# Bias of the masked softmax on ScalarE with v copied out first; the second block's value products moved and cut by token block

## The reference, cut to what matters

```python
# first block, per query block of 128 (dsa_attention)
rel   = relu(einsum('bqhd,bsd->bqhs', qi, ki))
score = einsum('bqh,bqhs->bqs', wi, rel)
score = where(visible, score, -inf)
_, idx = top_k(score, 128)
p = softmax(where(valid, (q @ k[idx]) * scale, -inf));  y_attn = p @ v[idx]
...
# second block (keys: 512 tokens and 16 meta tokens)
# out_a: 8 query heads over 2 key heads, plain softmax
p = softmax(qa @ ka * scale);  out_a = p @ va
# out_b: 4 heads, each with two softmaxes over the keys
p = softmax(qb @ kb * scale)                # two per head
w = p[:, :, 0] - lam * p[:, :, 1]
out_b = rms_norm(w @ vb, subln_g) * (1 - lam_init)
x = x + concat([out_a, out_b]) @ w_out      # then the feed-forward part
```

## Time and profile before

| what | value |
|---|---|
| median of 3 runs | 2317.85 us (2316.51 to 2325.55) |
| the profiled execution, its own time | 2319.75 us |
| its span | 2317.6 us |
| busy: PE, PEld, DVE, ACT, POOL | 98%, 78%, 44%, 26%, 63% |
| weight chunks loaded | 350 of 512 KB |

### The profile page before, as it was taken

The page is one execution under the profiler, slowest core; times in us unless marked ns, Lnnn a source line. Parts: engine busy times, 40 slices in busy tenths (PEclk is TensorE's granted clock), DMA queues, the critical chain, the costliest instruction groups (busy, mean ns, idle before and its releaser), DMA issues.

```text
span 2317.6 us, 30711 instructions
## 1 busy us (share of the span) xinstructions
PE 2261.8 (98%) x11027; PEld 1819.0 (78%) x11027; DVE 1016.3 (44%) x1568; ACT 609.1 (26%) x1081; POOL 1466.5 (63%) x1452
## 2 busy tenths in 40 slices
PE   8999999999999999999999999999999889999999
PEld 7767887888888887778878888888887557888887
DVE  6975654533321049658545332311483554323200
ACT  4333324221110023243242211110334553111100
POOL 6644765876766756548658676667492246766763
PEclk9999999999999999999999999999999999999999
DMA  5321233322222233213343222222320102222222
GB/s 184 100 73 55 96 109 123 127 91 100 96 94 100 94 113 105 68 56 102 103 141 117 94 97 93 100 91 100 119 106 10 37 1 91 93 98 100 93 98 82
DMA packets 69859, 217.35 MB, mean 94 GB/s; under 512 B 8448, under 2 KB 10752, under 8 KB 69632
## 3 DMA queue, kind: packets, MB, share of 16 engines
q1 hardware_dynamic: 54016, 188.41, 24.4%
q10 hardware_dynamic: 15744, 27.52, 3.3%
HBM read 195.93 MB, written 10.49 MB: 89 GB/s over the span
## 4 chain that ended last, share of the span: by engine, by line
PE 90%; DVE 6%; ACT 2%; issue 1%; DMA 0%; ACTq 0%; POOL 0%; DVEq 0%; POOLq 0%
PE ps L1673 79%; PE ps L2167 2%; PE ps L2000 1%; DVE score L1453 1%; DVE small L1449 1%; PE ps L1939 1%; ACT pe L1017 1%; PE ps L1924 1%; PE ps L2227 1%; PE ps L2229 1%; PE ps L2187 1%; PE ps L1952 1%; PE ps L1987 0%; PE ps L2030 0%; PE ps L2096 0%
## 5 line engine op out<-in xcount | busy, mean ns | idle before, releaser
L536 POOL TENSOR_TENSOR w_lo<-w_raw,w_hi 128x512 fp32r<-128x512 f32 x700 | 954.1, 1363 | 58.4
L533 POOL TENSOR_SCALAR w_hi<-w_raw 128x512 fp32r<-128x512 f32 x700 | 491.4, 702 | 658.6 <-DMA w_raw<-wst 628.4
L1673 PE MATMUL ps<-h_hi,w_lo 128*128 128x512 f32 (+1 forms) x2056 | 804.5, 391 | 18.7 <-ACT v_sb L786 4.0
L1673 PE MATMUL ps<-h_hi,w_hi 128*128 128x512 f32 (+1 forms) x2056 | 785.1, 382 | 0.0
L1673 PE MATMUL ps<-h_lo,w_hi 128*128 128x512 f32 (+1 forms) x2056 | 785.0, 382 | 0.0
L1673 PEld LDWEIGHTS ps<-h_hi,w_lo 128*128 128x128 f32 x2056 | 387.8, 189 | 120.4 <-issue 33.0
L1673 PEld LDWEIGHTS ps<-h_lo,w_hi 128*128 128x128 f32 x2056 | 387.9, 189 | 78.4 <-issue 6.7
L1673 PEld LDWEIGHTS ps<-h_hi,w_hi 128*128 128x128 f32 x2056 | 387.6, 189 | 75.0
L1673 PE MATMUL ps<-a_hi,w_lo 128*128 128x512 f32 (+1 forms) x572 | 213.7, 374 | 0.0
L1673 PE MATMUL ps<-a_hi,w_hi 128*128 128x512 f32 (+1 forms) x572 | 213.2, 373 | 0.0
L1673 PE MATMUL ps<-a_lo,w_hi 128*128 128x512 f32 (+1 forms) x572 | 213.2, 373 | 0.0
(11 more groups left out here) (304 smaller groups left out, 2535.4 us busy)
## 6 DMA issues: line engine op xcount, KB each, us to landing
w_raw<-wst SPq DMA_DIRECT2D x350, 512.0 KB, 3.5
rot<-raw ACTq DMA_DIRECT2D x70, 128.0 KB, 3.2
gates<-gt ACTq DMA_DIRECT2D x32, 256.0 KB, 4.1
stage<-gates ACTq DMA_DIRECT2D x32, 256.0 KB, 3.6
x_sb<-xin SPq DMA_DIRECT2D x8, 256.0 KB, 5.4
out<-x_sb SPq DMA_DIRECT2D x8, 256.0 KB, 4.5
kc<-cst ACTq DMA_DIRECT2D x1, 1056.0 KB, 5.1
kc<-cst SPq DMA_DIRECT2D x1, 417.0 KB, 8.0
```

What stands on the lines that cost most here:

```text
L533: eng.tensor_scalar(w_hi[s][:, part], w_raw[s][:, part], 1.0, 1.0, ALU.mult, ALU.mult)\
L536: eng.tensor_tensor(w_lo[s][:, part], w_raw[s][:, part], w_hi[s][:, part].bitcast(F32), ALU.subtract)\
L1673: m = eng.matmul(o, w, x, start=first and i == 0, stop=final and i == 2)
```

## The change

Four things:

1. In the first block ACT copies v0 to v3 out ahead of `qk_norm(7)` instead of behind it.
2. The bias is made on ACT, as Relu(score x 5e-9 + 1e30), so 1e30 where a key was not kept and 0 where it was; DVE subtracts it. It stands ahead of the copy of f3 and waits for the last MATCH_REPLACE (`topk_done`); DVE's first reduction of each query block waits for it (`bias_ready`). The copy of the causal mask is on ACT too.
3. In the second block the pieces of `VB_FILLS` are spread otherwise: steps 0 to 4 have 3, 3, 1, 1, 0 of them (before 4, 4, 3, 3, 2), steps 6 to 12 have the same number as before, and steps 14 to 16 have 2, 3, 3 (before none). The values of units 4 to 7 are multiplied by one query block at a time, one block per step (`values_differential`).
4. `kept_split` comes 4 steps later (t = 19 to 21, before 15 to 17), and `result_lower` of these one step behind it instead of in the same step. The output projection takes k in the order 3, 0, 1, 2, 4, ...

```diff
-VB_FILLS = {0: (1, range(0, 4)), 1: (1, range(4, 8)), 2: (2, range(0, 3)), 3: (2, range(3, 6)), 4: (2, range(6, 8)),
...
+VB_FILLS = {0: (1, range(0, 3)), 1: (1, range(3, 6)), 2: (1, range(6, 7)), 3: (1, range(7, 8)),
...
+            14: (4, range(0, 2)), 15: (4, range(2, 5)), 16: (4, range(5, 8))}
+KEPT_AT = TB * PAIRS_A + 3
+SPLIT_ORDER = [3, 0, 1, 2, 4, 5, 6, 7]
...
+def values_before(u, b):
+
+    return 2 * u + b // 2 + 1 if u < PAIRS_A else 2 * PAIRS_A + TB * (u - PAIRS_A) + b + 1
...
-                qk_norm(7)
                 for t in range(TB):
                     free(eng.activation(v_sb[:, t, :], acc((l, f"v{t}")), ACT.Copy), (l, f"v{t}"))
+                qk_norm(7)
+
+                def bias(b):
+
+                    dst = bias_t[:, BOFF[b]:BOFF[b] + NKEYS[b]]
+                    if b == 0:
+                        eng.activation(dst, causal, ACT.Copy, scale=-1.0).then_inc(bias_ready, 1)
+                        return
+                    eng.wait_ge(topk_done, 3 * l + b)
+                    eng.activation(dst, score[:, b - 1, 0:NKEYS[b]], ACT.Relu, scale=NEG / -2.0e38, bias=far)\
+                       .then_inc(bias_ready, 1)
+
                 for i in range(4):
+                    if i == 3:
+                        for b in range(TB):
+                            bias(b)
                     free(eng.activation(f_sb[:, i, :], acc((l, f"f{i}")), ACT.Copy), (l, f"f{i}"))
...
-                for b in (1, 2, 3):
-                    after(last[b])
-                    k = step(eng.tensor_scalar(bias_t[:, BOFF[b]:BOFF[b] + NKEYS[b]], score[:, b - 1, 0:NKEYS[b]],
-                                               -2.0e38, NEG, ALU.is_gt, ALU.mult))
-                after(k)
...
+                        if p == 0 and i == 0:
+                            eng.wait_ge(bias_ready, 4 * l + b + 1)
...
-                    eng.wait_ge(v2_done, 2 * u - 1 + b // 2)
+                    eng.wait_ge(v2_done, values_before(u - 1, b))
...
-                if 0 <= t - TB * PAIRS_A + 1 < KEPT:
-                    kept_split(t - TB * PAIRS_A + 1)
+                if 0 <= t - KEPT_AT < KEPT:
+                    kept_split(t - KEPT_AT)
...
-                if 0 <= t - TB * PAIRS_A + 1 < KEPT:
-                    result_lower(t - TB * PAIRS_A + 1)
+                if 0 <= t - KEPT_AT - 1 < KEPT:
+                    result_lower(t - KEPT_AT - 1)
...
+            def values_differential(u, b):
+
+                eng.wait_ge(t2_taken[b % 2], turns_before(u) + b // 2 + 1)
+                if b == 0 and u == PAIRS_A:
+                    eng.wait_ge(ysp_lo, 8 * L2 + 1)
+                    taken(eng, (L2, "vbm"))
+                elif b == 0:
+                    eng.wait_ge(y2_taken, u - PAIRS_A)
+                cols = slice((u - PAIRS_A) * P, (u - PAIRS_A + 1) * P)
+                toks = slice(b * P, (b + 1) * P)
+                y = bank(7)
+                for kb in range(TB):
+                    m = eng.matmul(y[:, toks], vb_sb[:, kb, cols], pt2[0][:, kb, toks], start=b + kb == 0, stop=False)
+                m.then_inc(v2_done, 1)
+                if b == TB - 1:
+                    eng.wait_ge(tm_taken, u + 1)
+                    eng.matmul(y, vbm_sb[0:META, cols], ptm[0:META, :], start=False, stop=True).then_inc(y2_ready, 1)
...
-                if b == 0 and u > 0:
+                if b == 0 and 0 < u <= PAIRS_A:
                     values(u - 1, 1)
-                if b == 2 and u >= 0 and u < UNITS:
+                if b == 2 and 0 <= u < PAIRS_A:
                     values(u, 0)
+                if t - LAG - 1 >= TB * PAIRS_A:
+                    values_differential(*divmod(t - LAG - 1, TB))
```

More of the change, by code:

```diff
@@ L1096, in _ @@
             step(eng.memset(eps, EPS))
+            step(eng.memset(far, -NEG))
             eng.wait_ge(in_dma, 32)
@@ L1445, in _ @@
                 for i in range(8):
-                    for _ in range(2):
+                    for j in (2 * i, 2 * i + 1):
                         for b in (1, 2, 3):
@@ L1452, in _ @@
                             s = score[:, b - 1, 0:NKEYS[b]]
-                            last[b] = step(eng.match_replace(s, m8[b], s, MARK))
-                    rope(3 + i)
-                for b in (1, 2, 3):
-                    after(last[b])
-                    k = step(eng.tensor_scalar(bias_t[:, BOFF[b]:BOFF[b] + NKEYS[b]], score[:, b - 1, 0:NKEYS[b]],
-                                               -2.0e38, NEG, ALU.is_gt, ALU.mult))
-                after(k)
+                            ins = eng.match_replace(s, m8[b], s, MARK)
+                            if j == TOPK // 8 - 1:
+                                ins.then_inc(topk_done, 1)
+                            else:
+                                last[b] = step(ins)
+                    rope(3 + i)
                 for p in range(PAIRS_1):
@@ L2206, in values @@
                 for i in range(2):
-                    eng.wait_ge(t2_taken[i], turns_before(u) + (2 * j + 2 if u < PAIRS_A else j + 1))
+                    eng.wait_ge(t2_taken[i], turns_before(u) + 2 * j + 2)
                 if j:
@@ L2212, in values @@
                     eng.wait_ge(vz_dma, 16)
-                elif u <= KEPT:
+                else:
                     eng.wait_ge(y2_kept, u)
[L2215 to L2219, removed]
                 rows = [slice(64 * i, 64 * i + 64) for i in range(2)]
-                cols = slice((u - PAIRS_A) * P, (u - PAIRS_A + 1) * P)
                 toks = HALVES[j]
@@ L2224, in values @@
                 for kb in range(TB):
[L2225 to L2229, removed]
+                    for i in range(2):
+                        m = eng.matmul(y[rows[i], toks], va_sb[:, kb, rows[i]], pt2[i][:, kb, toks], start=j + kb == 0, stop=False)
                 m.then_inc(v2_done, 1)
-                if j == 0:
-                    return
-                if u < PAIRS_A:
+                if j:
                     for i in range(2):
                         m = eng.matmul(y[rows[i]], vmz[0:2 * META, rows[i]], ptm[0:2 * META, :], start=False, stop=True)
-                else:
-                    m = eng.matmul(y, vbm_sb[0:META, cols], ptm[0:META, :], start=False, stop=True)
-                m.then_inc(y2_ready, 1)
+                    m.then_inc(y2_ready, 1)
+            def values_differential(u, b):
[14 more added lines that the diff above has]
+                    eng.matmul(y, vbm_sb[0:META, cols], ptm[0:META, :], start=False, stop=True).then_inc(y2_ready, 1)
             def o_square_2(h):
@@ L2264, in _ @@
             cs = [chunk((L2, f"wo{i}")) for i in range(4)]
-            for k in range(KT):
-                if k == 2:
+            for n, k in enumerate(SPLIT_ORDER):
+                if n == 2:
                     o_square_2(HH - 1)
-                eng.wait_ge(ysp_lo, 8 * L2 + k + 1)
+                eng.wait_ge(ysp_lo, 8 * L2 + n + 1)
                 for i in range(4):
-                    m = product(bank(i), *weights(cs[i], k), h_hi[:, k, :], h_lo[:, k, :], k == 0, k == KT - 1)
-                    if k == KT - 1:
+                    m = product(bank(i), *weights(cs[i], k), h_hi[:, k, :], h_lo[:, k, :], n == 0, n == KT - 1)
+                    if n == KT - 1:
                         m.then_inc(w_used, 1)
```

23 lines of the change are left out of this document (13 added, 10 removed).

## The result

The changed kernel takes 2304.36 us (median of 6, 2301.65 to 2307.34) against 2318.61 of the kernel before (median of 6), a ratio of 0.9937 with a 95% interval of 0.9923 to 0.9951. The forecast was 2304.4. The profiled execution has a span of 2303.3 us; that of before had 2317.6.

The account below looks back on a forecast made before the run. PE, with 90% of the span, was taken to bound the kernel. Gains of 2.4 (layer 0), 3.1 (layer 1) and 8.0 (second block) sum to 13.5 us, from 2317.85 to 2304.4, range 2300.5 to 2310.5.

Parts of the forecast that it names:

- Early steps +4.1: Second block's attention, steps 0 to 4: with fewer value pieces they take 18.2 us against 22.4, a gain of 4.1.
- Steps 14 and 15 -2.1: Second block's attention: two and three value pieces more in these steps cost 1.40 and 0.74 us, a loss of 2.1.
- Steps 16 and 17 -0.1: Second block's attention: step 16 with three more pieces plus step 17 at the floor, 9.74 us against 9.63.
- Step 18 +1.6: Second block's attention: DVE's copy no longer stands behind ACT's split, so a 1.58 us wait goes, gain 1.6.
- Steps 21 to 31 +1.8: Values by blocks: meta-key steps gain 1.0, steps behind lose 0.5 to 0.6; +0.4 in two units, +1.0 at step 30.
- The loop's end (+1.0): Behind the attention loop: only one value block left before the output projection, gain 1.0 us, from -0.5 to 1.6.
- layer 0 (2.4 of 4.0): First block, layer 0: fill(0) earlier by 2.4 us if the clock falls again as before, 4.0 if not.
- layer 1 (3.1): First block, layer 1: PE's wait for v and the half-clock stretch behind it go, scores 3.1 us earlier.
- Step 20: Second block's attention: 5.25 us with values at half clock becomes 3.5 with values by blocks, gain 1.7.
- the clock case: Rival: new half-clock stretches behind waits in both layers and at the loop's end, gain 9.5 to 12, about 2306.9; chance 0.24.
- the dear blocks: Rival: narrow value blocks in the second block's attention cost 1.92 us each, time 2314.7, halfway 2310; chance 0.08.
- the slower case: Rival: PE held at the lower clock in the later attention steps, 30 us over fifteen steps, 2334; chance 0.05.

Follow-up runs that it names:

- e1_layers: Kernel before with items 1 and 2 alone (v copied first, bias on ACT in the first block): 2312.78 us, ratio 0.9974.
- e9_projection_in_gap: Changed kernel with twelve matmuls of the output projection's tile 0 put into PE's wait at the loop's end: 2299.30 us, ratio to before 0.9919.
- e12_no_spread: Changed kernel with the table of value pieces (VB_FILLS) of the kernel before: 2305.34 us, ratio 0.9939.
- e10_after_again: The changed kernel itself, the same program measured once more: 2302.95 us (2301.38 to 2304.32).
- e7_late_split: Kernel before with item 4 alone (later splits): 2314.97 us, ratio 0.9976.
- e3_v_first: Kernel before with v copied out ahead of qk_norm(7), bias still on VectorE: 2317.22 us, ratio 0.9989.

## Why the prediction was right

The total (13.5 forecast, 14.3 measured) is right, and so are these terms singly. Early steps +4.1: 3.99. Steps 14 and 15 -2.1: -2.12. Steps 16 and 17 -0.1: -0.09. Step 18 +1.6: 1.65. Steps 21 to 31 +1.8: 2.21, though by two errors that cancel in part: the steps with the meta keys gave 0.84 each for the 1.0, and those behind them lost 0.14 for the 0.5 to 0.6. And the value block, taken at 0.9 from the earlier trace rows with 1.92 as its upper bound: 1.00 from its start to that of the transposes, 1877.96 to 1878.96. The Trainium skill's spacings (TensorE: Matmul & The Clock Gate, section on the back-to-back issue gap), from which the prediction had estimated a block near 1.92, did not carry over to these float32 products.

The loop's end (+1.0) reads 0.62 in the two profiles. Over the traces step 31 to the projection takes 15.2 to 16.4 us with two blocks, 15.6 on average, and 14.6 to 14.7 with single ones: 0.9, as forecast. What the prediction put at nothing is the half-clock stretch that ran on behind the projection's start in three of the six older traces (21.0 us from there to the residual in all others, 22.3 to 23.7 in these), another 0.9 on average.

Three steps hold less than the total suggests.

*The clock in the two layers.* I let the half-clock stretch stand in layer 0 (2.4 of 4.0) and fall away in layer 1 (3.1). The trace had it the other way round: 3.76 and 1.65. That their sum is right, 5.4 against 5.5, is luck of the execution. The mistake is not the choice of layer, but that I chose by layer at all. The traces show that it comes and goes with the execution: in the five traces that have both edits and an unsplit fill(0) (the changed kernel twice, e1, e9, e12), rope to fill is 2.9 eight times of ten and 4.2 twice. In the five that have neither edit it is 5.4 to 6.8, on average 6.2. The change's worth is thus about 3.0 us a layer, 6.0 in both, near the 5.9 of e1_layers. The 0.8 that the table shows as lost again before each residual is hardly work of the change: fill(0) to the first residual takes 284.5 to 286.9 us in layer 0 without the edits and 284.8 to 286.0 with them, 283.8 to 284.9 and 284.1 to 285.2 in layer 1. In the changed trace PE has a wait of 0.98 us there at 389.45, in a stretch where POOL's split of the next chunk had itself waited 10.21 us for the chunk's load; e10_after_again has no such wait there, but one of 0.52 in layer 1. What sets these waits was not tried and stays open.

*Step 20 (+1.7, measured 1.56).* Right in size for these two profiles, but it was counted as a sure gain of "values by blocks": e1_layers and e7_late_split have the old blocks of two and 3.6 us in that step. Where it took 5.2 the values ran at half clock, as the prediction had read, and by these traces that is worth 1.1 on average (1.6 in four of six). Four of six traces with old blocks had it and none of eight with new ones, so the blocks may make it rarer; that is not shown.

*The sum's grouping.* I credited the spread with 4.1 and the later split with 1.6. By e7_late_split the later split alone frees 1.99 in steps 16 and 17 and 1.65 in step 18, 3.6 in all, and the spread then pays 2.1 for the pieces it puts into step 16. The line "-0.1" hid both. As a sum it was right, but a reader of it would have kept the wrong half.

One thing came in from outside: the startup's 1.04 and the norm's 1.5 are in the difference of the two profiled executions (14.3) and not of the change. Against these 2.5 us stand the two losses behind the layers (0.83, 0.76) and layer 1's half-clock stretch (1.3), 2.9 together, and a loop's end 1.2 short of its average. That the difference of the two executions is near that of the medians all the same is luck. The rivals: the clock case was right in mechanism, came in one layer, and at the loop's end in every trace of the changed kernel (1.3 by e9_projection_in_gap); the dear blocks fell; the slower case fell, with the scores at 1.24 to 1.31 throughout steps 19 to 30 and no half-clock stretch there. The Trainium skill (TensorE: Matmul & The Clock Gate, its part on the clock gate) has the change of level vary from run to run; with e10_after_again beside the first trace, this case agrees.

## What to carry to other kernels

Where two engines' paths meet, an edit on one of them can measure as next to nothing (1.5 us each here, 5.9 together); read both paths at the join (end of the rotary step, last copy, bias) and move them together. Before spreading work over a loop of steps with a floor, add up what each step would take at both ends of the move: here the early gain of 4.0 us was paid back in full later, and the gain lay in the wait that a neighbouring edit took away. When a wait of the bounding engine can't be shortened, fill it with work that is ready and that nobody needs yet: 2.7 us of products in a 3.3 us gap were worth 4.0, of which 1.3 is the half-clock stretch behind the gap.

## What the runs showed of the hardware

At the norm near 1634 us, the same instructions behind the same 1.9 us wait of PE took 5.8 us in six traces and 7.3 in eight, with the granted clock 1.00 in one and 0.57 in the other. Here the changed kernel and then e12_no_spread, over four microseconds each:

```profile
1633.70:1637.70 4.00, 3.98 (x33) 4.00 (x34) 3.88 (x10) 2.07 (x5) 0.00 (x0) 1.00 0.30 116
```

```profile
1633.00:1637.00 4.00, 4.00 (x23) 4.00 (x22) 3.74 (x11) 2.35 (x6) 0.00 (x0) 0.57 0.06 26
```

Where two traces differ by one such stretch it costs 1.3 to 1.6 us, and a longer one more (3.2 at the loop's end of e3_v_first against before). The trace of before has five of them; that of e9_projection_in_gap, whose gap is filled, has none before its last microseconds. Over the fourteen traces each of them, but for those in the last microseconds of the program, stands at a wait of PE of 1.3 to 3.5 us. The 3.3 to 3.5 us wait at the loop's end brought one in all twelve traces that have it; the waits of 1.3 to 2.1 us brought one in some and not in others, and what decides that stays open. The end of layer 0's `rope(10)`, which nothing in these edits reaches, moved by up to 3.9 us between traces. So the difference of two single profiles of this kernel is uncertain by several microseconds, while a step or a join that no half-clock stretch falls into reproduces to 0.02.
